# Seven additions of squares behind each post-norm: from VectorE's queue to GpSimd's

## The reference, cut to what matters

```python
mix = einsum('bsd,de->bse', merged, w_out)
x = x + rmsnorm(mix, norm_mix_post)            # first place
h = rmsnorm(x, norm_ffn_pre)
gu = einsum('bsd,df->bsf', h, w_ffn_up)
...
ff = einsum('bsf,fd->bsd', silu(gate) * up, w_ffn_down)
x = x + rmsnorm(ff, norm_ffn_post)             # second place
h = rms_norm(x, norm_g_2);  proj = einsum('bsd,de->bse', h, w_in_2)
```

## Time and profile before

| | us |
|---|---|
| median of 3 runs | 1084.9 (1082.96 to 1084.91) |
| the profiled execution, its own time | 1083.51 |
| its span, first to last instruction | 1081.8 |
| TensorE busy | 1055.8 (98%) |
| VectorE busy | 518.3 (48%) |
| GpSimd busy | 518.9 (48%) |
| ScalarE busy | 457.5 (42%) |

### The profile page before, as it was taken

One profiled execution on the slowest core, in us unless ns is written; L12 is line 12 of the kernel. 1 busy time (PEld: TensorE's weight loads), 2 busy tenths in 40 slices (PEclk: granted clock), 3 DMA queues, 4 the chain that ended last, 5 costly groups with the idle time before them and its releaser, 6 DMA issues.

```text
span 1081.8 us, 13309 instructions
## 1 busy us (share of the span) xinstructions
PE 1055.8 (98%) x4926; PEld 872.9 (81%) x4926; DVE 518.3 (48%) x801; ACT 457.5 (42%) x666; POOL 518.9 (48%) x300
## 2 busy tenths in 40 slices
PE   6999999999999999999999999999999999999898
PEld 5888887888888787888888888887778878888786
DVE  5799773563362555434343410007324467566621
ACT  5322336788552433333332322224434437557620
POOL 3344554944344424444444464452576445546543
PEclk9999999999999999999999999999999999999999
DMA  6222221121142313222222323332122211111111
GB/s 222 97 98 96 81 98 39 41 77 59 59 156 97 117 39 98 97 97 97 97 97 97 97 98 102 112 106 89 59 87 71 76 59 49 35 54 40 39 62 75
DMA packets 25965, 91.03 MB, mean 84 GB/s; under 512 B 3008, under 2 KB 3136, under 8 KB 25792
## 3 DMA queue, kind: packets, MB, share of 16 engines
q1 hardware_dynamic: 25920, 90.42, 24.7%
HBM read 88.31 MB, written 2.10 MB: 84 GB/s over the span
## 4 chain that ended last, share of the span: by engine, by line
PE 93%; DVE 3%; issue 2%; ACT 1%; POOL 1%; DMA 0%; SPq 0%; DVEq 0%; POOLq 0%; ACTq 0%
PE ps L420 29%; PE ps L421 28%; PE ps L422 28%; PE ps L828 1%; PE ps L555 1%; PE ps L462 1%; PE ps L549 1%; DVE s L1937 1%; PE ps L449 1%; DMA w_raw<-weights 0%; POOL w_lo L2090 0%; PE ps L886 0%; PE ps L739 0%; PE ps L740 0%; PE ps L755 0%
## 5 line engine op out<-in xcount | busy, mean ns | idle before, releaser
L2090 POOL TENSOR_TENSOR w_lo<-w_raw,w_hi 128x1024 fp32r<-128x1024 f32 x147 | 351.3, 2390 | 437.4 <-ACT w_hi L1001 388.1
L1001 ACT ACTIVATE w_hi<-w_raw 128x1024 fp32r<-128x1024 f32 x141 | 147.4, 1046 | 299.6 <-PE ps L422 299.0
L420 PE MATMUL ps<-a_hi,w_hi 128*128 128x512 f32 x560 | 224.1, 400 | 14.8 <-DVE w_lo L1501 7.0
L422 PE MATMUL ps<-a_hi,w_lo 128*128 128x512 f32 x560 | 219.4, 392 | 0.0
L421 PE MATMUL ps<-a_lo,w_hi 128*128 128x512 f32 x560 | 219.3, 392 | 0.0
L420 PE MATMUL ps<-b_hi,w_hi 128*128 128x512 f32 x416 | 163.8, 394 | 6.6 <-issue 5.4
L421 PE MATMUL ps<-b_lo,w_hi 128*128 128x512 f32 x416 | 163.1, 392 | 0.0
L422 PE MATMUL ps<-b_hi,w_lo 128*128 128x512 f32 x416 | 162.9, 392 | 0.0
L420 PEld LDWEIGHTS ps<-a_hi,w_hi 128*128 128x128 f32 x560 | 105.9, 189 | 40.0 <-issue 8.9
L422 PEld LDWEIGHTS ps<-a_hi,w_lo 128*128 128x128 f32 x560 | 105.8, 189 | 23.0
L421 PEld LDWEIGHTS ps<-a_lo,w_hi 128*128 128x128 f32 x560 | 106.2, 190 | 20.7
(11 more groups left out here) (321 smaller groups left out, 1652.2 us busy)
## 6 DMA issues: line engine op xcount, KB each, us to landing
w_raw<-weights SPq DMA_DIRECT2D x159, 512.0 KB, 3.2
resid<-x_t SPq DMA_DIRECT2D x8, 256.0 KB, 5.3
resid<-x_t SPq DMA_DIRECT2D x1, 2048.0 KB, 9.1
out_t<-out_sb SPq DMA_DIRECT2D x8, 256.0 KB, 2.0
w_raw<-weights SPq DMA_DIRECT2D x2, 256.0 KB, 4.4
vec<-vecs SPq DMA_DIRECT2D x1, 220.0 KB, 8.7
vec<-vecs SPq DMA_DIRECT2D x1, 4.0 KB, 1.6
```

Of the source, the lines that this page charges most:

```text
L420: pe.matmul(out, s_hi, m_hi, start=first, stop=False, skip_group_check=True)
L422: return pe.matmul(out, s_lo, m_hi, start=False, stop=last, skip_group_check=True)
L1001: act.activation(w_hi[:, k % 2, 0:width], w_raw[:, k, 0:width], ACT.Copy).then_inc(hi_ready, 1)
L2090: pool.tensor_tensor(w_lo[:, k % 2, 0:width], w_raw[:, k, 0:width], w_hi[:, k % 2, 0:width].bitcast(F32), ALU.subtract).then_inc(lo_ready, 1)
```

## The change

VectorE's `new_residual` loses its seven additions. GpSimd gets a function `add_squares`, which for c = 1 to 7 waits for square c (`sq_ready`), adds it to square 0's tile, and lets each addition wait for the one before it by a semaphore of its own; the last raises `acc_ready`. It stands in GpSimd's queue behind the low part of U_UP+3 (U_Q2+3) and ahead of those of U_UP+4 and U_UP+5 (U_Q2+4 and U_Q2+5). Nothing else moves.

```diff
-                for c in range(1, KC):
-                    add_square(sq, n_sq, c)
                 norm(q + 1, D, r_exp)
...
+            summed = Steps(pool, squares_summed)
+
+            def add_squares(sq, n_sq):
+
+                for c in range(1, KC):
+                    pool.wait_ge(sq_ready, n_sq + c + 1)
+                    if c > 1:
+                        summed.wait()
+                    add = pool.tensor_tensor(sq[:, 0, :], sq[:, 0, :], sq[:, c, :], ALU.add)
+                    if c < KC - 1:
+                        summed.do(add)
+                    else:
+                        add.then_inc(acc_ready, 1)
...
-            for n in range(U_UP + 2, U_UP + 6):
+            for n in range(U_UP + 2, U_UP + 4):
+                low_unit(n)
+            add_squares(sq_m, 2 * KC + CC)
+            for n in range(U_UP + 4, U_UP + 6):
                 low_unit(n)
...
-            for n in range(U_Q2 + 2, U_Q2 + 6):
+            for n in range(U_Q2 + 2, U_Q2 + 4):
+                low_unit(n)
+            add_squares(sq_f2, 4 * KC + CC)
+            for n in range(U_Q2 + 4, U_Q2 + 6):
                 low_unit(n)
```

More of the change, by code:

```diff
@@ L278, in two_layer_block @@
             sem("drs_ready"), sem("d_final"), sem("att2_final"), sem("mixed_ready"))
+        squares_summed = sem("squares_summed")
         pool_held, gap_zeroed = sem("pool_held"), sem("gap_zeroed")
@@ L1778, in copy_tiles, with new_residual @@
                     dve.tensor_copy(dst[:, j, :], ps[:, j % 4, :]).then_inc(tile_drained, 1)
-            def new_residual(q, src, sq, n_sq, gain_post, gain_next, dst_hi, dst_lo, n_hi, r_exp):
+            def new_residual(q, src, gain_post, gain_next, dst_hi, dst_lo, n_hi, r_exp):
                 norm(q, D, r_exp)
@@ L1804, in _ @@
             dve.wait_ge(x_again, 16)
-            new_residual(1, mix, sq_m, 2 * KC + CC, "g_mix_post", "g_ffn_pre", b_hi, b_lo, 2 * KC + CC, r_exp2)
+            new_residual(1, mix, "g_mix_post", "g_ffn_pre", b_hi, b_lo, 2 * KC + CC, r_exp2)
             def up_pairs(i, banks):
@@ L1830, in _ @@
             copy_tiles(ffo, sq_f, 3 * KC + CC)
-            new_residual(3, ffo, sq_f2, 4 * KC + CC, "g_ffn_post", "g_2", a_hi, a_lo, 3 * KC + CC + FC, r_exp3)
+            new_residual(3, ffo, "g_ffn_post", "g_2", a_hi, a_lo, 3 * KC + CC + FC, r_exp3)
             for k in range(4):
```

## The result

Over 20 runs each the changed kernel takes 1086.28 us in the median (1083.01 to 1088.31) against 1083.16 (1080.73 to 1085.65): ratio 1.0025, 95% interval 1.0016 to 1.0033. It is slower by 2.7 us by that ratio and by 3.1 us by the medians, where 3.6 were forecast. The profiled execution took 1085.55 us.

What follows compares the result with a forecast made beforehand. TensorE, 93% of the chain, was taken as the bound: removing VectorE's additions gains nothing, GpSimd's holds on VectorE cost 1.8 us a place, 3.6 for both. 1084.9 + 3.6 = 1088.5 us; range 1084.0 to 1092.7.

Steps and rivals of the forecast that it cites:

- The first step: At both places TensorE's sum needs VectorE's additions 3.4 us after they end, so removing their 5.46 us gains nothing.
- GpSimd's own time: GpSimd, idle from 367.53 to 391.03, keeps up with additions of 1.29 us; its new waits hold nothing up.
- The mechanism: A VectorE instruction with two SBUF inputs (R, L) is held until GpSimd's ends; M, which reads PSUM, is not.
- The prediction's 6.5 us: Whole cost if a 0.115 us handover gap replaced the 1.16 us used, making a pair of additions cost 1.97 us.
- The order of arrival: Addition 1 arrives at 373.10, 0.06 us after R(2) starts at 373.04; the same order returns at every odd addition.
- the walk: Step-by-step timing of the first place: two additions delay VectorE 1.49 us, chunk 7 starts 1.8 us late; chance 0.50.
- the rival in which every residual is held: Each addition comes ahead of R: chunk 7 4.6 us late, 9.2 us for both places, 1094.1 on the median; chance 0.15.
- the rival in which VectorE keeps its turn: Additions get in only at M; low parts 1.9 us late, under the 2.78 margin; 1083.5 to 1084.9 us; chance 0.22.
- the few tenths ahead of chunks 1, 3 and 5: TensorE should wait a few tenths of a us for low parts ahead of these chunks, about 1.0 us ahead of chunk 6.
- The size: A held R or L ends 0.61 us after the addition; 1.8 us lost at one place, 3.6 us at both.
- The absolute 1088.5: The whole time in us forecast from the median of the runs: 1084.9 + 3.6.
- The clock: TensorE's clock should stay at its upper 2.4 GHz, since its longest new idle time is near 1.0 us.

Runs made afterwards that it cites:

- e1: The changed kernel with the seven additions left out on both engines and the norm taken from chunk 0 alone; ratio 0.9997 to the kernel before.
- e3: The kernel before plus seven GpSimd memsets of about 1.3 us, which read nothing from SBUF, each behind a square; ratio 0.9995 to before.
- e2: The kernel before, VectorE's additions kept, plus seven GpSimd additions of the same form on two tiles nobody else uses; ratio 1.0153 to before.
- e7: The kernel before plus seven GpSimd stand-in additions on unshared tiles, with 256 columns in place of 512; ratio 1.0094 to before.
- e6: The changed kernel with ScalarE's square placed ahead of its high part; ratio 1.0017 to the kernel before.
- e4: The changed kernel with GpSimd adding only squares 1 to 4, VectorE adding 5 to 7 behind its last low part; ratio 1.0013 to before.
- e8: The kernel before with each low part ahead of the next residual on VectorE and 13 filling matmuls instead of 15; ratio 1.0074 to before.
- e5: The changed kernel with all of GpSimd's additions waiting for the last square; ratio 1.0074 to the kernel before.
- e9: The kernel before plus 256-column GpSimd stand-in additions, with GpSimd's next low parts waiting until VectorE's additions have ended; ratio 0.9983 to before.

## Why the prediction was right, point by point

**What bounds the kernel.** The first step, that nothing on the chain waits for the additions, is shown by e1: with none at all the stretch is 21.88 us as before, and the ratio's interval, 0.9985 to 1.0009, holds 1.

**GpSimd's own time.** Right: the seventh addition ends at 391.12 and the low part behind it starts at 392.71, at once when ScalarE delivers. e3 shows that so much time on GpSimd costs nothing here.

**The mechanism.** Right, and shown from three sides: the hold comes with foreign tiles (e2), not with instructions that read nothing (e3), and shrinks with half the columns (e7: 1.23 instead of 1.79 us). The Trainium skill ("SBUF — State Buffer", Who interferes with whom) says that a VectorE instruction with two SBUF inputs contends with a GpSimd instruction that reads SBUF and not with one that only writes it. The trace agrees: 0.74 us for L(1) beside the memset. The 0.115 us of the Trainium skill ("SBUF — State Buffer", A bandwidth-pool intuition that's wrong), measured there on a DMA whose descriptors GpSimd writes behind a VectorE copy, does not appear between these instructions: addition 1 ends at 375.26, 1.16 us after R(2)'s end at 374.10, which is less than its own 1.29. The prediction's 6.5 us has that figure in one of the two handovers only; in both, an estimate from this figure of the Trainium skill, on the same page, would be 2.5 us a pair and 9.6 us in all.

**The order of arrival.** Right: R(2) starts at 373.35, addition 1 at 373.41, the 0.06 us of the walk; the same at additions 3 and 5 within a hundredth (R(4) at 378.81 and 378.87 on GpSimd, R(6) at 384.27 and 384.34). So the rival in which every residual is held did not come. Nor did the rival in which VectorE keeps its turn: GpSimd gets in ahead of L(1), though a semaphore wait stands before it, satisfied since the high part ended at 372.81. Only one sign failed: of the few tenths ahead of chunks 1, 3 and 5, TensorE waited 0.2 us ahead of chunk 1, and chunks 3 and 5 started at their own pace (381.45 and 386.92).

**The size.** One term was too large: a held instruction was to end 0.61 us after the addition; it ends 0.55 after it (375.81 against 375.26 for L(1), 377.51 against 376.96 for R(3)). A pair then costs 1.36 us instead of 1.49, and the low part of chunk 6 is 4.1 late instead of 4.5. Chunk 6 starts 16.33 us after chunk 0 where the walk had 16.77, the idle time before it is 0.70 instead of 1.0, and a place costs 1.4 us instead of 1.8. Two places at 1.38 are 2.76 us where the forecast had 3.6. The whole time's 3.1 at equal clock comes nearer to 3.6 by luck: 0.4 of it lies outside the span, which the prediction had at nothing. The absolute 1088.5 was also built on a median of three runs, 1084.9, that lay 1.7 above the median of 20; together with the 0.9 of the size that is the distance to 1086.28, less the 0.4.

**The clock.** Right for the two places: 1.00 in windows over both stretches. The ground it stood on was thinner than it looked: the same idle time on TensorE is met by either level. In before one of 0.94 us ends at 919.12 and the clock from 920 to 922 is 1.00; in e1 one of 0.93 us ends at 919.16 and it is 0.50. So one trace with 1.00 behind 1.20 us could not rule a loss out. That the executions differ by some microseconds through the clock elsewhere was not in the prediction; the 1.4 us between the profiled execution and the median is part of that spread.

**What was not seen.** VectorE's additions of before end 0.08 us ahead of GpSimd's low parts. I read both numbers for the margin of the sum (3.44 us) and not for this. It did not matter for the change, which removes one of the two parties, but it decides what else may be moved at this place: 1.8 us of delay on VectorE, harmless to the chunks, cost 0.9% in e7.

## What to carry to other kernels

A VectorE instruction with two SBUF tensor inputs and a GpSimd instruction that reads SBUF did not run together here, but for 0.1 to 0.2 us at the handover: before work is moved from one to the other, lay both timelines over each other, give each meeting its price, and prefer slots in which VectorE reads PSUM (0.53 us a meeting in e6 against 1.36 for two; in the whole time that gain was not clear). Compare the sum of the prices with the margin of the first consumer, chunk by chunk: below it TensorE did not wait (e7's chunks), above it it did (e4 at chunk 1, the change at chunk 6). And look at the end of what is delayed as well as at its reader: the additions were 3.4 us early for TensorE, and 0.1 us from colliding with GpSimd's next work.

## What the runs showed of the hardware

- The two take turns by instruction: in e8 the rows alternate, and VectorE's seven additions, 5.46 us when alone, took 9.41 us beside two GpSimd instructions of 2.39 us. In e2 and e7, with a stand-in beside them too, they took 10.52 and 9.96.
- GpSimd pays as well: its addition of 1.29 us took 1.85 and 1.50 us when it met VectorE, 1.30 when it came first (e6).
- Two idle times of TensorE of 0.84 and 1.25 us, with only the sum's eight small matmuls between them, were followed by a clock of 0.51 over 3 us (e5); one idle time of 1.20 us amid full work was not the earlier trace rows, and one of 0.93 us was in e1, while its like of 0.94 in before was not.
- Between executions of mean clock 0.994 and 0.998 the kernel before differs by 4.6 us, more than the change under study. Much of the low clock stands behind one idle time of 3.48 us, which the traces show with 1.00 behind it (e9) and with 0.50 (before); some traces have a low stretch elsewhere too (e1 near 920).
